# RWKV-7 chunk products of a decoder step on all four 64x64 quarters of the matmul array

## The reference, cut to what matters

```python
def step(s, inp):
    r_t, w_t, k_t, v_t, kk_t, a_t = inp
    sa = jnp.einsum('bhij,bhj->bhi', s, -kk_t)
    s = (s * w_t[:, :, None, :] + sa[..., None] * (kk_t * a_t)[:, :, None, :]
         + v_t[..., None] * k_t[:, :, None, :])
    return s, jnp.einsum('bhij,bhj->bhi', s, r_t)
```

## Time and profile before

| | us |
|---|---|
| median of three runs | 904.88 (904.15 to 908.27) |
| profiled execution, its own time | 907.78 |
| its span, first to last instruction | 906.1 |
| PE busy | 881.9 (97%) |
| DVE busy | 639.3 (71%) |
| ACT busy | 450.2 (50%) |
| PE matmul records | 8588 |

### The profile page before, as it was taken

How to read it: one execution, slowest core, us unless ns; L and a number is a source line. 1 busy time by engine, 2 the same in 40 slices (tenths; PEclk the granted TensorE clock), 3 DMA queues, 4 the chain that set the end, 5 groups by cost and what they waited for, 6 DMA issues and landing times.

```text
span 906.1 us, 21269 instructions
## 1 busy us (share of the span) xinstructions
PE 881.9 (97%) x8588; PEld 768.6 (85%) x8588; DVE 639.3 (71%) x1083; ACT 450.2 (50%) x771; POOL 61.9 (7%) x95
## 2 busy tenths in 40 slices
PE   5999999999999999999899999999999999999998
PEld 4999899998998787877556899977998899889986
DVE  5564277656665974886824753799879887988796
ACT  6432545412332388886525425544674467436741
POOL 0000111213510000000000001010100000000000
PEclk9999999999999999999999999999999999999999
DMA  8443687853220569679987336787788433444343
GB/s 278 154 134 109 146 180 207 246 106 92 77 62 3 196 219 363 227 242 339 364 333 276 101 94 172 200 242 216 211 225 270 140 118 114 146 138 121 109 145 145
DMA packets 73163, 164.47 MB, mean 182 GB/s; under 512 B 5918, under 2 KB 32126, under 8 KB 70890
## 3 DMA queue, kind: packets, MB, share of 16 engines
q1 hardware_dynamic: 59370, 124.26, 39.8%
q0 software_dynamic: 13696, 38.85, 18.1%
HBM read 156.55 MB, written 40.10 MB: 217 GB/s over the span
## 4 chain that ended last, share of the span: by engine, by line
PE 85%; DVE 7%; DMA 4%; ACT 2%; issue 2%; SPq 0%; DVEq 0%; ACTq 0%; POOLq 0%
PE PS L982 16%; PE PS L984 16%; PE PS L983 16%; PE PS L1174 8%; PE PS L1337 5%; PE PS L1359 3%; PE PS L1409 2%; PE PS L1015 2%; PE PS L1297 2%; PE PS L1445 2%; PE PS L1323 2%; DVE WL L2916 1%; PE PS L1314 1%; PE PS L1643 1%; PE PS L1642 1%
## 5 line engine op out<-in xcount | busy, mean ns | idle before, releaser
L983 PE MATMUL PS<-WL,U 128*128 128x512 f32 x224 | 87.6, 391 | 0.0
L982 PE MATMUL PS<-WH,U 128*128 128x512 f32 x224 | 87.5, 391 | 0.0
L2037 ACT ACTIVATE WH<-Wraw 128x1024 fp32r<-128x1024 f32 x56 | 57.8, 1054 | 51.7 <-DMA Wraw<-tau 21.2
L2916 DVE TENSOR_TENSOR WL<-Wraw,WH 128x1024 fp32r<-128x1024 f32 x56 | 66.8, 1218 | 7.3 <-ACT WH L2037 7.3
L1174 PE MATMUL PS<-AR 64*64 64x64 f32 x1912 | 61.2, 220 | 3.4 <-issue 1.6
L982 PE MATMUL PS<-WR,HR 128*128 128x384 f32 (+1 forms) x184 | 63.8, 347 | 0.8 <-issue 0.8
L1174 PEld LDWEIGHTS PS<-AR 64*64 64x64 f32 x1912 | 58.7, 135 | 6.0 <-issue 3.9
L982 PE MATMUL PS<-h2H,WH 128*128 128x288 f32 x208 | 61.5, 296 | 1.2 <-DVE rc L3038 1.2
L983 PE MATMUL PS<-h2L,WH 128*128 128x288 f32 x208 | 61.3, 295 | 0.0
L984 PE MATMUL PS<-h2H,WL 128*128 128x288 f32 x208 | 61.2, 294 | 0.0
L984 PE MATMUL PS<-WH,U 128*128 128x512 f32 x152 | 59.2, 390 | 0.0
(11 more groups left out here) (436 smaller groups left out, 2305.0 us busy)
## 6 DMA issues: line engine op xcount, KB each, us to landing
AR<-in_cache_kv SPq DMA_DIRECT2D x120, 384.0 KB, 5.0
tau<-in_w_mlp_down POOLq DMA_DIRECT2D x24, 1024.0 KB, 9.2
Wraw<-tau SPq DMA_DIRECT2D x16, 1024.0 KB, 4.8
Wraw<-in_w_mlp_up SPq DMA_DIRECT2D x14, 1024.0 KB, 5.6
Wraw<-in_w_mlp_down SPq DMA_DIRECT2D x12, 1024.0 KB, 5.1
W<-in_w_in SPq DMA_DIRECT2D x6, 1536.0 KB, 9.0
QK<-in_cache_kv SPq DMA_DIRECT2D x8, 384.0 KB, 5.6
AR<-in_x_prompt SPq DMA_DIRECT2D x4, 512.0 KB, 9.1
```

The source lines that it names most:

```text
L982: mm(out, lH, rH, start=start, stop=False, skip_group_check=skip)
L983: mm(out, lH, rL, start=False, stop=False, skip_group_check=skip)
L2037: f(piece_half(WH, r, d, h), piece_half(Wraw, r, d, h), ACT.Copy).then_inc(w_hi, 1)
L2916: tt(piece_half(WL, r, d, h), piece_half(Wraw, r, d, h), piece_half(WH, r, d, h).bitcast(F32), SUB).then_inc(w_lo, 1)
```

## The change

For every chunk with `exchanged(a, c)` (chunks 4 to 8 of a = 0, chunks 0 to 3 of a = 1) the two heads lie exchanged between partition halves in some slots, called INNER; in the others, OUTER, nothing is exchanged. A product whose operands are of one kind and whose result is of the other then runs, for such chunks, in the two quarters off the diagonal. `per_chunk` issues chunk c and c+4 one behind the other, and `CHUNK_0 = 256` shifts the place in PSUM so that chunks 0 to 3 and 4 to 8 lie in two banks. KQt, HT and all dXT go from OUTER to OUTER and stay on the diagonal. In levels 2 to 4 the chunk 8 is left out, on PE, DVE (masks, subtractions) and ACT.

The samples' products in U and Y are issued with the head innermost. Y is reordered: the parts from the state of exchanged chunks come first, then two plain chunks, then PE waits for its own increment `state_ps`, then plain and exchanged chunks alternate. Both SS steps are issued as one. On DVE the start of the inverse takes three masks, two of them on 64 partitions that move a head to the other half, instead of one on 128.

```diff
+        HALVES = (slice(0, 64), slice(64, 128))
+        CHUNK_0 = 256
+        def exchanged(a, c):
+            return (c >= 4) == (a == 0)
+        def rows_of(h, a, c, inner):
+            return HALVES[h ^ int(inner and exchanged(a, c))]
+        def level_chunks(lev):
+            return NCH if lev < 2 else NCH - 1
...
-            def per_chunk(base, a, A, B, chunks=range(NCH), start=True, stop=True):
-                for c in chunks:
-                    for h in (slice(0, 64), slice(64, 128)):
-                        last = mm(PS[h, base + c * CH:base + (c + 1) * CH], chunked(A)[h, a, c, :],
-                                  B(h, a, c) if callable(B) else chunked(B)[h, a, c, :], start=start, stop=stop)
+            def product(base, h, a, c, A, B, frm, to, start=True, stop=True, skip=False):
+                rows = rows_of(h, a, c, frm == INNER)
+                out = PS[rows_of(h, a, c, to == INNER), base + CHUNK_0 + c * CH:base + CHUNK_0 + (c + 1) * CH]
+                return mm(out, chunked(A)[rows, a, c, :], eye(rows) if B is None else chunked(B)[rows, a, c, :],
+                          start=start, stop=stop, skip_group_check=skip)
+            def paired(chunks):
+                return sorted(chunks, key=lambda c: (c % 4 + 4 * (c == 8), c))
+            def per_chunk(base, a, A, B, frm, to, chunks=range(NCH)):
+                for c in paired(chunks):
+                    for h in range(2):
+                        last = product(base, h, a, c, A, B, frm, to)
...
-                        per_chunk(base, a, 3, 2).then_inc(c_ps, 1)
+                        per_chunk(base, a, 3, 2, INNER, OUTER, chunks).then_inc(c_ps, 1)
-                            per_chunk(base, a, 8, 5).then_inc(c_ps, 1)
+                            per_chunk(base, a, 8, 5, OUTER, INNER, chunks).then_inc(c_ps, 1)
-                        per_chunk(base, a, 5, 8).then_inc(c_ps, 1)
+                        per_chunk(base, a, 5, 8, OUTER, OUTER, chunks).then_inc(c_ps, 1)
...
-                    for h in (slice(0, 64), slice(64, 128)):
-                        for b in range(DB):
-                            last = mm(PS[h, base + 8 * CH:base + 9 * CH], hexp[h, a, b, :], S0[h, a, b, :],
+                    for b in range(DB):
+                        for h in range(2):
+                            last = mm(PS[rows_of(h, a, 8, True), at:at + CH], hexp[HALVES[h], a, b, :], S0[HALVES[h], a, b, :],
...
+                    for c in swapped:
+                        state_part(base, a, c, c == (4 if a == 0 else 1))
+                    for c in plain[0:2]:
+                        chunk_part(base, a, c, 0, True)
+                        state_part(base, a, c, False)
+                        chunk_part(base, a, c, 1, False)
+                    pe.wait_ge(state_ps, a + 1)
+                    for i in range(max(len(swapped), len(plain) - 2)):
+                        for n in range(2):
+                            if i + 2 < len(plain):
+                                last = chunk_part(base, a, plain[i + 2], n, True)
+                                if n == 0:
+                                    state_part(base, a, plain[i + 2], False)
+                            if i < len(swapped):
+                                last = chunk_part(base, a, swapped[i], n, False)
...
-                                link(tt(chunked(8)[:, a], chunked(0)[:, a], mask64(R_L1T), MUL))
-                                link(tt(chunked(8)[:, a], id64, chunked(8)[:, a], SUB))
+                                first_inverse(a)
```

More of the change, by code:

```diff
@@ L364, in build @@
         c_ps = sem("c_ps")
+        state_ps = sem("state_ps")
         c_ev = sem("c_ev")
@@ L1181, in rwkv_products, with eye @@
+            def paired(chunks):
[4 more added lines that the diff above has]
+                        last = product(base, h, a, c, A, B, frm, to)
+                return last
+            def eye(rows):
+                return cst[rows, K_ID:K_ID + 128][:, rows]
+            OUTER, INNER = 0, 1
             def rwkv_products():
-                for kind, A, B in (("LT", 8, 1), ("L", 1, 8), ("ArbT", 8, 4), ("LkT", 3, 1), ("ArkT", 3, 4),
-                                   ("Vt", 6, eye), ("KQt", 1, eye), ("BEt", 9, eye), ("KEt", 5, eye)):
+                for kind, A, B, to in (("LT", 8, 1, INNER), ("L", 1, 8, INNER), ("ArbT", 8, 4, INNER), ("LkT", 3, 1, INNER),
+                                       ("ArkT", 3, 4, INNER), ("Vt", 6, None, INNER), ("KQt", 1, None, OUTER),
+                                       ("BEt", 9, None, INNER), ("KEt", 5, None, INNER)):
@@ L1210, in rwkv_products @@
                     base = begin("MT", a, "H")
[L1211 removed]
+                    per_chunk(base, a, 1, 17, INNER, OUTER, range(8)).then_inc(c_ps, 1)
                     yield
@@ L1214, in rwkv_products @@
                     base = begin("N", a, "G")
-                    for c in range(8):
-                        per_chunk(base, a, 18, 14, [c], stop=False)
-                        last = per_chunk(base, a, 17, 19, [c], start=False)
+                    for c in range(4):
+                        for cc in (c, c + 4):
+                            for h in range(2):
+                                product(base, h, a, cc, 18, 14, INNER, OUTER, True, False)
+                        for cc in (c, c + 4):
+                            for h in range(2):
+                                last = product(base, h, a, cc, 17, 19, INNER, OUTER, False, True)
                     last.then_inc(c_ps, 1)
@@ L1242, in rwkv_products, with state_part @@
                     yield
+                def state_part(base, a, c, start):
+                    swapped = [x for x in range(NCH) if exchanged(a, x)]
+                    if 1 <= c < 8:
+                        for h in range(2):
+                            last = product(base, h, a, c, 5, 4, OUTER, OUTER, start, False, exchanged(a, c))
+                    elif c == 8:
+                        for b in range(DB):
+                            c0 = SEQ + b * DT
+                            for h in HALVES:
+                                last = mm(PS[h, base + CHUNK_0 + c0:base + CHUNK_0 + c0 + DT], S0[h, a, b, :],
+                                          slot(4)[h, a, c0:c0 + DT], start=False, stop=False, skip_group_check=True)
+                    if c == swapped[-1]:
+                        last.then_inc(state_ps, 1)
@@ L1243, in rwkv_products, with chunk_part @@
+                def chunk_part(base, a, c, n, start):
+                    A, B = ((9, 11), (14, 12))[n]
+                    for h in range(2):
+                        last = product(base, h, a, c, A, B, INNER, OUTER, start and n == 0, n == 1, exchanged(a, c))
+                    return last
                 for a in range(2):
                     base = begin("Y", a, "U")
[L1245 to L1252, removed]
-                                    mm(PS[h, base + c0:base + c0 + DT], S0[h, a, b, :], slot(4)[h, a, c0:c0 + DT],
-                                       start=False, stop=False, skip_group_check=True)
-                        last = per_chunk(base, a, 14, 12, [c], start=False)
+                    swapped = [c for c in range(NCH) if exchanged(a, c)]
+                    plain = [c for c in range(NCH) if not exchanged(a, c)]
+                    for c in swapped:
[13 more added lines that the diff above has]
+                                last = chunk_part(base, a, swapped[i], n, False)
@@ L1258, in rwkv_products @@
                 pe.wait_ge(masked_ready, 4)
[L1259 to L1265 removed]
+                bases = [begin("SS", a) for a in range(2)]
+                for n, (A, wide) in enumerate(((17, uexp), (18, hexp))):
+                    for a in range(2):
+                        for h in range(2):
+                            rows = rows_of(h, a, 8, True)
+                            last = mm(PS[HALVES[h], bases[a]:bases[a] + 512], chunked(A)[rows, a, 8, :], wide[rows, a, :, :],
+                                      start=(n == 0), stop=(n == 1))
+                        if n == 1:
+                            last.then_inc(c_ps, 1)
+                yield
+                yield
                 for kind, src, after in (("GM", 6, "Y"), ("GV", 14, "GM")):
```

47 lines of the change are left out of this document (29 added, 18 removed).

## The result

The changed kernel takes 901.12 us (median of 6 runs, 897.33 to 902.98) beside 906.41 us for the kernel before in the same comparison: ratio 0.9937, 95% interval 0.9920 to 0.9954. Run once more on another chip it took 898.81 beside 907.33, ratio 0.9922 (0.9898 to 0.9946). The medians differ by 5.3 and 8.5 us; by the ratios the change is worth 5.7 us (4.2 to 7.3) and 7.1 us (4.9 to 9.3), and the two measurements overlap. The forecast 10.5 would be a ratio of 0.9884, outside both intervals. In absolute terms the forecast was 894.4 us with a range of 889.5 to 897.5; 1.5 us of the distance to 901.12 are the kernel before, whose median is 906.41 here and was 904.88 in the forecast. The profiled execution of the changed kernel took 901.0 us with a span of 899.3 (before: 907.78 and 906.1).

What follows compares the result with a forecast made beforehand. PE was taken to set the pace up to 281 us, DVE from 292.5 to 317. Savings 2.6+4.5+1.3+1.2+1.05+1.0 = 11.65, less 1.2 for new waits, gave 10.5: 904.9 - 10.5 = 894.4 us, range 889.5 to 897.5.

Steps and rivals of the forecast that it cites:

- Four quarters, slot 0.062, step 0.61: RWKV steps: one record on each of four quarters takes 0.062 us, so a nine-chunk step takes 0.61 instead of 1.05.
- floor of 25 ns: Rival, chance 0.12: each PE record costs at least about 25 ns, step 0.92 us, gain 6.2, so 898.7 us.
- in turn: Rival, chance 0.07: off-diagonal quarters run in turn with the others, slot 0.117 us, gain 3.2, so 901.7 us.
- collision: Rival, chance 0.05: row halves writing the same PSUM partitions in two banks collide, slot 0.16, 12.6 us slower, 917.5.
- Operand products, 2.6 less 0.6 for waits = 2.0: ArbT, LkT, ArkT, Vt, BEt, KEt: 12 steps save 0.22 us each, 2.6 us; LT, L and KQt save nothing.
- Levels, T1, H, G, MT, N, 6.4 net: Inverse levels save 4.5 us, T1, H, G 1.3, MT and N 1.2, before a part of the new waits.
- evacuation loop: Product, evacuation, product in the same place: about 1.65 us per two steps, 0.82 per step, bounding instead of the array.
- 1.6 more, may double: Inside the range only: PE's idle time for no engine, looking like missing instructions, may double, 1.6 us more.
- U and the stretch to 317 us, 2.05: U of a = 0 saves 1.05 us; from there to 317 us 1.0 is taken, DVE allowing at most 2.0.
- U's 1.05: U of a = 0 falls from 2.47 to 1.42 us, saving 1.05.
- Carried to the end: All of the 10.5 us gained at 317 us reaches the end; rival, lost later in page loads, 904.9, chance 0.06.
- What would show it: Signs: records 15 to 16 ns apart, PE idle before L1174 some 12 us, DVE near full, page load 9 to 11 earlier.

Runs made afterwards that it cites:

- e8_few: The changed kernel without the sample chunk's products in the 38 steps that still had them, 152 records less: 901.33 us, ratio 0.9927.
- the burst: The changed kernel with 1024 unread records of 64 columns over four quarters put in where the RWKV steps begin: these took 28.2 us.

## Why the prediction was wrong

- *Four quarters, slot 0.062, step 0.61:* right, 0.058 and 0.62. So were the diagnosis that up to the sequential steps PE sets the pace, and three rivals' rejection: no floor of 25 ns (14.4 and 14.9 measured), not in turn (29), no collision (over 32). That the floor's 898.7 and the 901.7 of quarters in turn lie near the two measured medians is chance. (In the sum from which the collision would decide, the six dXT steps, which stay on the diagonal, should not have been counted; it changes 0.128 by less than 0.001.)
- *Operand products, 2.6 less 0.6 for waits = 2.0:* 1.8 to 2.2 measured. No wait for "issue" falls in this stretch, the first ends at 227.14 us: the records that are ready at the start and the waits at L cover it.
- *Levels, T1, H, G, MT, N, 6.4 net:* 4.1 and 5.7 measured. **This step failed.** The forecast had taken weight loads 7 ns apart as how fast instructions can come; that holds for what is fetched already. Sustained, 128 records cost 3.73 to 4.01 us, so a step of 36 takes 1.05 to 1.13 us, no less than the 1.05 of the kernel before, instead of the evacuation loop's 0.82. The forecast knew of it as "1.6 more, may double"; measured, "issue" took 5.7 us up to the sequential steps and 1.0 in Y, 5.1 more than before. Not all of it is lost, as a later evacuation hides behind it.
- *U and the stretch to 317 us, 2.05:* 1.0 and 0.4 measured. **The second step that failed**, in size. DVE was named as the bound with at most 2.0 from 292.5 us. By the stage it is 27.0 - 24.1 = 2.9 at most from U on, and DVE can't be filled: six kernels stand at 25.8 us with 24.1 of work, so 1.2 was the most. Crediting U's 1.05 in full beside the bounded rest was the error: U and Y did become 3.4 to 3.6 us faster and 2.6 to 3.0 were waited away behind them.
- *Clock, no term:* stretches at the lower clock came; L took 0.7 us longer in one, and no run shows that they cost the program anything of their own.
- *Carried to the end:* right. From the keys' transposes on 585.31 and 583.30 us beside 584.42; the first load of a page starts at 288.67 instead of 297.49, 8.8 us earlier (forecast 9 to 11).
- *What would show it:* records 15 to 16 ns apart, and a larger idle time before L1192 (11.2 us instead of 3.4), both came true. But half of that idle time had no engine behind it.

Still open: how much of the levels' shortfall is supply and how much evacuation, and what DVE's stretch would give with less work in it. The two measurements of the changed kernel can't be told apart by their intervals, but seq differs by 2.0 us between its two profiles, with the same instructions; packets of instructions took 0.9 to 1.8 us there, which may be part of it, and was not tried. No order tried beat the changed kernel by more than the measurement can tell.

## What to carry to other kernels

Price code of short matmuls twice: by the array, and by instructions, here 128 matmuls with their weight loads per 3.7 to 4.0 us once some 256 are used up. A faster array pays in bursts or where long instructions lie between; beyond that, only fewer instructions do, and only until the next bound: 64 records of left-out zero products, with shorter evacuations beside them, brought 2 us or more, and 152 further records less (e8_few) brought nothing clear. The kernel before was at that pace already. And where a second engine has nine tenths of a stretch to do, credit a saving of the first only down to what the second needs by itself, gaps between its instructions included: here 25.8 us for 24.1 of work, on two quarters and on four.

## What the runs showed of the hardware

- Four 64x64 quarters, of which the two that write the same partitions write different banks, run in full side by side: 14.4 to 14.9 ns per record of 64 columns, about 22 for 96 (7.76 us for 346, waits apart), 27.2 for 128 ((10.71-0.28)/383). The two on the diagonal do so in one bank: 512 records in 15.15 us, 29.2 ns each.
- Instructions arrive for PE in packets of 16 KB; when it waits for them, the 128 records of each start 3.73 to 4.01 us behind those of the last, and that where other DMA is small (share 0.03 in the first 4 us of the burst).
- Below 64 columns a quarter gains nothing: records of 16 columns on one quarter start 59 ns apart at clock 1.00. The granted clock fell to the lower level 3.6 us into that run of records, without idle time before it, and of the 51.82 us for 512 nearly all lie there (columns as in the earlier trace rows):

```profile
365.70:417.40 51.70, 51.70 (x513) 51.70 (x512) 0.00 (x0) 0.00 (x0) 0.00 (x0) 0.53 0.01 1
```
